# Another VectorE order in the folded down stages of a two-block fp32 network, and narrower weight panels

## The chip, the cores and the metric

One core of a Trainium2 chip runs the whole program. The metric is device time in microseconds (us); lower is better.

## What is computed

Two network blocks run one after the other on an fp32 activation of 512 tokens by 1024 features. The first is a gated mixer with a feed-forward layer, the second a short-convolution mixer, a forgetting attention and two convolutional feed-forward layers. The lines that matter here are the down projections of the feed-forward layers:

```python
h = rmsnorm(x, norm_ffn[l])
x = x + jnp.square(jax.nn.relu(h @ w_ff1[l])) @ w_ff2[l]
...
def conv_ffn(xn, w_up, conv_w, w_down):
    up = xn @ w_up
    a, g = jnp.split(up, 2, axis=-1)
    a = causal_dwconv(a, conv_w)
    return (jax.nn.silu(a) * g) @ w_down
```

The first layer has 4096 hidden features, each of the two others 2816.

## The kernel before

**Tiles and panels.** Activations lie transposed, 128 features by 512 tokens to a tile. Each fp32 operand is split in a high part (rounded to `fp32r`) and a low part (what is left), and a product takes three matmuls: high by high, high by low, low by high. The weights come as 353 panels of 128 x 1024. SyncE loads a panel into one of three slots (`w_raw`), ScalarE makes the high half (`high`, L478), GpSimd the low half (`low`, L433), TensorE reads both. ScalarE works `FEED` = 2 panels ahead. In the code `p0` is the first panel of a stage, and the stage's pair j has the panels p0 + 2j and p0 + 2j + 1.

**Folded down stages.** The hidden features are worked off in chunks of 8 tiles (the last chunk of each conv layer has 6): an up stage makes the hidden tiles, and a down stage adds their product to `x`. Eight of the down stages are folded (`FOLDED`): three of ff1, two of the first and three of the second conv layer. In such a stage two weight panels and the two halves of the tokens form a 2 x 2 block product, which is worked out with seven block products instead of eight. A stage has four pairs of panels (j = 0 to 3), so 28 blocks of 12 matmuls of 256 columns (9 in the last stage). For each pair:

- VectorE first makes four sums of weight quadrants. `sum_first` (L1069) overwrites a quadrant in `w_raw`, after ScalarE has copied the old one to PSUM (`copy_a21`, L523). `sum_third` (L1078) and `sum_rest` (L1084, L1086) write to PSUM. ScalarE makes the high halves of three of them (`high_of_sum`), VectorE the low halves (`low_of_sum`, L1092).
- TensorE works seven blocks. Blocks 1, 5 and 7 go to one PSUM accumulator, and between them VectorE must read it: `add_first` (L1147) after block 1, `add_second` (L1164) after block 5, `add_third` (L1182) after block 7. Block 5 waits for `add_first`, block 7 for `add_second`.
- Blocks 2 and 3 go to a second bank, read by `add_sides` (L1155, L1156), blocks 4 and 6 to a third, read by `add_crossing` (L1173). Block 4 of the next pair waits for the crossing.

All sums and additions are VectorE's, in an order that is written out by hand: `last_tile` has what comes with the last hidden tile and pair 0, `down_pairs` the rest. ScalarE's order is in its own `down_pairs`.

**The ring.** A load waits until the low half of the panel three before is made; the first panel of a pair is also a source of the sums, so the load over it (`load`, L388 to L392) waits for the pair's last sum. Since SyncE issues loads in order, the next one stands behind it:

```python
                    sp.wait_ge(w_low, p - RING + 1)
                    if PAIR_OF.get(p - RING, (0, 1))[1] == 0:
                        sp.wait_ge(s_made, 4 * PAIR_OF[p - RING][0] + 4)
```

So the sums of pair 1 gate the load of panel p0 + 5, the second of pair 2. On ScalarE and GpSimd a high or low half also waits until TensorE has read its slot (`wait_slot`).

Of the kernel before, what the change touches and what calls it, by code (L numbers as in the profile page):

```python
# [8 lines left out]
P = 128  # L9
SEQ = 512  # L10
D = 1024
DT = D // P
# [56 lines left out]
for _p in PAIRS:  # L69
    PAIR_OF[_p], PAIR_OF[_p + 1] = (PAIR_AT[_p], 0), (PAIR_AT[_p], 1)  # L70
WHOLE = [sum(1 for _i in range(_p + 1) if _i not in PAIR_OF) for _p in range(N_PANELS)]


B1_HIGH, T_HIGH, PART_LOW, REST_LOW = {}, {}, {}, {}
# [62 lines left out]
def build(nc, xT, panels, const, late, param, rows, ws, outT):  # L137
# [5 lines left out]
    with ctx:  # L143
# [241 lines left out]
        @block.sync  # L385
        def _(sp):
            def load(p):
                if p >= RING:  # L388
                    sp.wait_ge(w_low, p - RING + 1)
                    if PAIR_OF.get(p - RING, (0, 1))[1] == 0:  # L390
                        sp.wait_ge(s_made, 4 * PAIR_OF[p - RING][0] + 4)
                sp.dma_start(w_raw[:, p % RING, :], panels[p]).then_inc(w_in[p % RING], 16)  # L392

            sp.dma_start(params[:], param).then_inc(param_in, 16)
            for m in range(DT):
                sp.dma_start(x[:, m, :], xT[m]).then_inc(x_in[m], 16)
                if m == 0:
                    load(0)
            load(1)
            load(2)  # L400
            sp.dma_start(consts[:], const).then_inc(c_in, 16)
            for p in range(RING, N_PANELS):
                load(p)
                if p == RING + 1:
                    sp.dma_start(rows_sb, rows.partition_broadcast(P)).then_inc(row_in, 16)
                    sp.dma_start(ws_sb, ws).then_inc(row_in, 16)
                m = p - (S["upb"] + RING + 1)
                if 0 <= m < DT:

                    sp.wait_ge(evicted, S["upb"] + m + 1)  # L410
                    sp.dma_start(x[:, m, :], xT[m]).then_inc(x_again[m], 16)
                    if m == 0:
                        sp.dma_start(consts[:, LATE:LATE + N_LATE], late).then_inc(late_in, 16)
            for m in range(DT - 1):

                sp.wait_ge(evicted, N_PANELS - DT + m + 1)
                sp.dma_start(outT[m], x[:, m, :]).then_inc(out_done, 16)

            for part in range(2):
                at = slice(part * SEQ // 2, (part + 1) * SEQ // 2)  # L420
                sp.wait_ge(evicted, N_PANELS + part)
                sp.dma_start(outT[DT - 1][:, at], x[:, DT - 1, at]).then_inc(out_done, 16)
            sp.wait_ge(out_done, 16 * (DT + 1))

        @block.gpsimd
        def _(pool):
            def low(p):

                if p >= N_PANELS:
                    return  # L430
                pool.wait_ge(w_high, p + 1)
                wait_slot(pool, p)
                nc.gpsimd.tensor_tensor(w_lo[:, p % RING, :], w_raw[:, p % RING, :], w_hi[:, p % RING, :].bitcast(F),  # L433
                                        ALU.subtract).then_inc(w_low, 1)


            def low_t23(key, i):

                k2 = TILES_AT[key] // 2
                pool.wait_ge(t_high, T_HIGH[key] + k2 + 2 * i + 1)  # L440
                nc.gpsimd.tensor_tensor(t23_lo[:, i, :], keep[i], t23_hi[:, i, :].bitcast(F),
                                        ALU.subtract).then_inc(t23_low, 1)

            def low_t23_behind(p):

                for key in FOLDED:
                    p0, tiles = down_stage(*key)
                    k2 = tiles // 2
                    if key[0] == "ff1":
                        ready = {p0 - DT + 2 + m: m - 1 for m in range(5, 8)}  # L450
                        if p in ready:
                            low_t23(key, ready[p] - k2)
                        if p == p0 + 1:
                            low_t23(key, k2 - 1)
                    else:
                        m = (p - 3 - (p0 - 2 * tiles)) // 2
                        if p % 2 == (p0 + 1) % 2 and k2 <= m < tiles:
                            low_t23(key, m - k2)

            pool.wait_ge(x_low, DT)  # L460
            for p in range(N_PANELS):
                low(p)
                low_t23_behind(p)

        @block.scalar
        def _(act):
            steps = Steps(act, act_steps)

            def high(p):

                if p >= N_PANELS:
                    return
                if PAIR_OF.get(p, (0, 0))[1] == 1:
                    act.wait_ge(s_made, 4 * PAIR_OF[p][0] + 1)
                else:
                    act.wait_ge(w_in[p % RING], 16 * (p // RING + 1))
                wait_slot(act, p)
                nc.scalar.copy(w_hi[:, p % RING, :], w_raw[:, p % RING, :]).then_inc(w_high, 1)  # L478

            def split(dst, src, scale=None):  # L480
                return nc.scalar.activation(dst, src, ACT.Copy, scale=1.0 if scale is None else scale)  # L481
# [43 lines left out]
            def down_pairs(key):  # L525

                p0, tiles = down_stage(*key)
                for j in range(DT // 2):
                    p = p0 + 2 * j
                    more = j < DT // 2 - 1  # L530
                    if j > 0:
                        if more:
                            copy_a21(PAIR_AT[p + 2], tiles)
                        high(p + FEED)
                    high(p + FEED + 1)
                    if more:
                        for i in range(3):
                            high_of_sum(PAIR_AT[p + 2], i, tiles // 2 * P)
# [477 lines left out]
        def _(dve):  # L1016
# [126 lines left out]
            def add_first(p0, j):  # L1143
# [2 lines left out]
                dve.wait_ge(part_made, 7 * q + 1)  # L1146
                v.tensor_tensor(x[:, m, 0:HALF], x[:, m, 0:HALF], acc_of(p0, j), ALU.add).then_inc(acc_read, 1)  # L1147

            def add_sides(p0, j):

                q, m = PAIR_AT[p0 + 2 * j], 2 * j
                p5 = ps[:, SIDE_BANKS[0], HALF:SEQ]
                dve.wait_ge(part_made, 7 * q + 3)
                dve.wait_ge(acc_read, 2 * q + (1 if j > 0 else 2))
                v.tensor_tensor(x[:, m, :], x[:, m, :], ps[:, SIDE_BANKS[0], :], ALU.add).then_inc(side_read, 1)  # L1155
                v.tensor_tensor(x[:, m + 1, HALF:SEQ], x[:, m + 1, HALF:SEQ], p5, ALU.add).then_inc(side_read, 1)  # L1156

            def add_second(p0, j):

                q, m = PAIR_AT[p0 + 2 * j], 2 * j  # L1160
                dve.wait_ge(part_made, 7 * q + 5)
                if j > 0:
                    dve.wait_ge(side_read, 2 * q + 2)
                v.tensor_tensor(x[:, m, HALF:SEQ], x[:, m, HALF:SEQ], acc_of(p0, j), ALU.add).then_inc(acc_read, 1)  # L1164

# [23 lines left out]
            def last_tile(key, to):  # L1189

                p0, tiles = down_stage(*key)
                q, i, k2 = PAIR_AT[p0], tiles // 2 - 1, tiles // 2
                low_rest(key, i, to, k2)
                t2_t3(key, i, k2)
                if key[0] == "ff1":
                    low_of_sum(q, 0, tiles)
                low_of_sum(q, 1, tiles)
                add_first(p0, 0)
                t4(key, i, k2)
                sum_first(q + 1, tiles)  # L1200
                low_t4(key, i, k2)
                low_of_sum(q, 2, tiles)

            def down_pairs(key):

                p0, tiles = down_stage(*key)
                for j in range(DT // 2):
                    q = PAIR_AT[p0 + 2 * j]
                    more = j < DT // 2 - 1
                    if j == 0:  # L1210
                        add_second(p0, j)
                        add_sides(p0, j)
                        add_crossing(p0, j)
                        sum_third(q + 1, tiles)
                        sum_rest(q + 1, tiles)
                        low_of_sum(q + 1, 0, tiles)
                        low_of_sum(q + 1, 1, tiles)
                        continue
                    low_of_sum(q, 2, tiles)
                    add_third(p0, j - 1)  # L1220
                    if more:
                        sum_first(q + 1, tiles)
                    add_first(p0, j)
                    if more:
                        sum_third(q + 1, tiles)
                        sum_rest(q + 1, tiles)
                    add_sides(p0, j)
                    if more:
                        low_of_sum(q + 1, 0, tiles)
                    add_second(p0, j)  # L1230
                    if more:
                        low_of_sum(q + 1, 1, tiles)
                    add_crossing(p0, j)
# [1213 lines left out]
```

## Time and profile before

| | before |
|---|---|
| median of 3 runs | 2032.32 us (2031.04 to 2032.36) |
| profiled execution | 2033.78 us |
| its span | 2032.0 us |
| mean granted clock of TensorE | 0.997 |
| HBM read, written | 190.62 MB, 2.10 MB |
| loads of weight panels | 353 of 512 KB |

The span runs from the first to the last instruction; what lies around it is the start and the end of the execution. Times in the rows further on are microseconds from the start of the span.

### The profile page before, as it was taken

To read this page: it belongs to the slowest core of one execution; us is meant where nothing else is said; L and a number is where in the kernel's file an instruction comes from. 1 tells how busy PE (TensorE), PEld (TensorE's weight loads), DVE (VectorE), ACT (ScalarE), POOL (GpSimd) and SP (SyncE) were. 2 spreads that over 40 slices of the span, in tenths; PEclk is the share of its full clock that TensorE was granted. 3 is DMA by queue.
4 is the path that set the end of the run, shared out by engine and by line. 5 is a ranking of instruction groups with operands and counts; after the bars stand their busy time and mean duration, and the time that the engine had idled before them with its cause. 6 is when DMAs were issued, how large, how long until landed. Compare 5 with 4: busy or idle time off the path is not lost. (4 is left out here: it accounts for less than half of the span.)

```text
span 2032.0 us, 28871 instructions
## 1 busy us (share of the span) xinstructions
PE 2005.0 (99%) x11386; PEld 1696.0 (83%) x11386; DVE 1203.8 (59%) x1985; ACT 908.2 (45%) x1389; POOL 909.7 (45%) x388
## 2 busy tenths in 40 slices
PE   9999999999999999999999999999999999999998
PEld 7888888888889888888888889888877778888987
DVE  4688888634737454434457557454376746755657
ACT  6455556534534434512434234246377743423333
POOL 4334443644545444444445445454422234545544
PEclk9999999999999999999999999999999999999999
DMA  5222222433333232332322333332311122332323
GB/s 179 82 86 74 84 84 83 131 133 93 100 98 104 84 104 94 101 95 86 103 93 94 104 94 108 92 117 88 104 53 63 52 84 94 98 100 94 105 92 104
DMA packets 55286, 194.59 MB, mean 96 GB/s; under 512 B 6128, under 2 KB 6640, under 8 KB 55152
## 3 DMA queue, kind: packets, MB, share of 16 engines
q1 hardware_dynamic: 55152, 192.75, 29.7%
q8 instruction: 91, 1.49, 0.3%
q14 instruction: 43, 0.35, 0.1%
HBM read 190.62 MB, written 2.10 MB: 95 GB/s over the span
## 5 line engine op out<-in xcount | busy, mean ns | idle before, releaser
L433 POOL TENSOR_TENSOR w_lo<-w_raw,w_hi 128x1024 fp32r<-128x1024 f32 x353 | 869.9, 2470 | 1045.6 <-ACT w_hi L478 1029.3
L1860 PE MATMUL ps<-a_hi,w_hi 128*128 128x512 f32 x1152 | 456.4, 396 | 0.2 <-DVE x L1245 0.2
L1862 PE MATMUL ps<-a_hi,w_lo 128*128 128x512 f32 x1152 | 449.1, 390 | 0.0
L1861 PE MATMUL ps<-a_lo,w_hi 128*128 128x512 f32 x1152 | 448.8, 390 | 0.0
L478 ACT CAST w_hi<-w_raw 128x1024 fp32r<-128x1024 f32 x353 | 365.0, 1042 | 144.9 <-PE ps L1884 58.3
L1860 PE MATMUL ps<-b_hi,w_hi 128*128 128x512 f32 x1000 | 390.1, 390 | 0.2 <-DVE x L1245 0.2
L1862 PE MATMUL ps<-b_hi,w_lo 128*128 128x512 f32 x1000 | 389.1, 389 | 0.0
L1861 PE MATMUL ps<-b_lo,w_hi 128*128 128x512 f32 x1000 | 389.0, 389 | 0.0
L1034 DVE TENSOR_TENSOR arena<-ps,inv_rms 128x512 f32<-128x512 f32 x176 | 121.4, 690 | 309.6 <-PE ps L1862 292.0
L1860 PEld LDWEIGHTS ps<-a_hi,w_hi 128*128 128x128 f32 x1152 | 216.3, 188 | 47.8 <-issue 2.8
L1861 PEld LDWEIGHTS ps<-a_lo,w_hi 128*128 128x128 f32 x1152 | 216.4, 188 | 45.7 <-issue 2.2
L1862 PEld LDWEIGHTS ps<-a_hi,w_lo 128*128 128x128 f32 x1152 | 216.2, 188 | 45.3
L1860 PEld LDWEIGHTS ps<-b_hi,w_hi 128*128 128x128 f32 x1000 | 187.7, 188 | 39.8 <-issue 1.0
L1862 PEld LDWEIGHTS ps<-b_hi,w_lo 128*128 128x128 f32 x1000 | 187.7, 188 | 39.2
L1861 PEld LDWEIGHTS ps<-b_lo,w_hi 128*128 128x128 f32 x1000 | 187.7, 188 | 38.8 <-issue 0.2
L481 ACT ACTIVATE a_hi<-arena 128x256 fp32r<-128x256 f32 (+1 forms) x70 | 35.0, 508 | 169.9 <-DVE arena L1634 67.1
L845 ACT ACTIVATE ps<-ps 128x512 f32<-128x512 f32 x44 | 25.6, 582 | 186.0 <-DVE ps L1625 186.0
L481 ACT ACTIVATE s_hi<-ps 128x512 fp32r<-128x512 f32 (+1 forms) x96 | 52.7, 584 | 95.2 <-PE ps L1884 48.5
L1882 PE MATMUL ps<-t_hi,s_hi 128*128 128x256 f32 x248 | 72.1, 291 | 19.7 <-DVE x L1147 14.6
L1092 DVE TENSOR_TENSOR s_lo<-ps,s_hi 128x512 fp32r<-128x512 f32 (+1 forms) x96 | 62.7, 669 | 33.1 <-ACT s_hi L481 33.1
L1883 PE MATMUL ps<-t_lo,s_hi 128*128 128x256 f32 x248 | 70.8, 286 | 0.0
L1884 PE MATMUL ps<-t_hi,s_lo 128*128 128x256 f32 x248 | 70.3, 284 | 0.0
(277 smaller groups left out, 3142.1 us busy)
## 6 DMA issues: line engine op xcount, KB each, us to landing
w_raw<-in_panels SPq DMA_DIRECT2D x353, 512.0 KB, 3.6
x<-in_xT SPq DMA_DIRECT2D x16, 256.0 KB, 2.8
outT<-x SPq DMA_DIRECT2D x7, 256.0 KB, 3.1
consts<-in_const SPq DMA_DIRECT2D x1, 528.5 KB, 8.2
arena<-in_rows SPq DMA_DIRECT2D x1, 256.0 KB, 4.6
arena<-in_ws SPq DMA_DIRECT2D x1, 256.0 KB, 5.1
outT<-x SPq DMA_DIRECT2D x2, 128.0 KB, 1.8
consts<-in_late SPq DMA_DIRECT2D x1, 168.0 KB, 2.6
```

Of the source, the lines that this page charges most:

```text
L433: nc.gpsimd.tensor_tensor(w_lo[:, p % RING, :], w_raw[:, p % RING, :], w_hi[:, p % RING, :].bitcast(F), ALU.subtract).then_inc(w_low, 1)
L478: nc.scalar.copy(w_hi[:, p % RING, :], w_raw[:, p % RING, :]).then_inc(w_high, 1)
L481: return nc.scalar.activation(dst, src, ACT.Copy, scale=1.0 if scale is None else scale)
L845: nc.scalar.activation(hidden(m), hidden(m), ACT.Silu).then_inc(silu_done, 1)
L1034: return v.tensor_tensor(dst, bank(p), inv_rms[:, :], ALU.mult)
L1092: v.tensor_tensor(s_lo[:, i, 0:h], ps[:, S_BANKS[i], 0:h], s_hi[:, i, 0:h].bitcast(F), ALU.subtract).then_inc(s_low, 1)
L1860: nc.tensor.matmul(o, wh, hi[:, kt, :], start=(kt == 0), stop=False)
L1861: nc.tensor.matmul(o, wh, lo[:, kt, :], start=False, stop=False)
L1862: ins = nc.tensor.matmul(o, wl, hi[:, kt, :], start=False, stop=(kt == tiles - 1))
L1882: nc.tensor.matmul(o, wh, rh, start=(first and kt == 0), stop=False, skip_group_check=not first)
L1883: nc.tensor.matmul(o, wh, rl, start=False, stop=False, skip_group_check=not first)
L1884: ins = nc.tensor.matmul(o, wl, rh, start=False, stop=(kt == k2 - 1), skip_group_check=not first)
```

## The change

There are three parts. `COLS` gives each panel a width: the 16 panels of the two 6-tile down stages get 768 columns in place of 1024, in the load, the high half and the low half. ScalarE's order in pair 1 gets `high(p + FEED)` ahead of `copy_a21`. And VectorE's order changes in pairs 0, 1 and 2 of each folded stage.

```diff
+COLS = [D] * N_PANELS
+for _l, _n in [(_l, _n) for _l in range(2) for _n in range(len(FF2_CHUNKS))]:
+    _p0, _tiles = down_stage(f"ffn_{_l}", _n)
+    COLS[_p0:_p0 + DT] = [_tiles * P] * DT
...
-                sp.dma_start(w_raw[:, p % RING, :], panels[p]).then_inc(w_in[p % RING], 16)
+                sp.dma_start(w_raw[:, p % RING, 0:COLS[p]], panels[p][:, 0:COLS[p]]).then_inc(w_in[p % RING], 16)
...
-                    if j > 0:
+                    if j == 1:
+                        high(p + FEED)
+                        copy_a21(PAIR_AT[p + 2], tiles)
+                    elif j > 0:
                         if more:
                             copy_a21(PAIR_AT[p + 2], tiles)
                         high(p + FEED)
...
+            def sides_first(p0, j):
+                return j > 0 or p0 < S["conv_b"]
...
                 add_first(p0, 0)
                 t4(key, i, k2)
+                if sides_first(p0, 0):
+                    add_sides(p0, 0)
                 sum_first(q + 1, tiles)
                 low_t4(key, i, k2)
                 low_of_sum(q, 2, tiles)
...
                     if j == 0:
                         add_second(p0, j)
+                        sum_third(q + 1, tiles)
+                        sum_rest(q + 1, tiles)
+                        if not sides_first(p0, j):
+                            add_sides(p0, j)
+                        low_of_sum(q + 1, 0, tiles)
+                        add_crossing(p0, j)
+                        low_of_sum(q + 1, 1, tiles)
+                        continue
+                    low_of_sum(q, 2, tiles)
+                    add_third(p0, j - 1)
+                    if more:
+                        add_first(p0, j)
+                        sum_first(q + 1, tiles)
                         add_sides(p0, j)
-                        add_crossing(p0, j)
+                        add_second(p0, j)
                         sum_third(q + 1, tiles)
                         sum_rest(q + 1, tiles)
                         low_of_sum(q + 1, 0, tiles)
                         low_of_sum(q + 1, 1, tiles)
+                        add_crossing(p0, j)
                         continue
-                    low_of_sum(q, 2, tiles)
-                    add_third(p0, j - 1)
```

Pair 3 keeps its order. `sides_first` is true in pair 0 of the ff1 stages only (and in all later pairs).

VectorE in the first folded stage, from `add_first` of pair 0 to `add_second` of pair 1. Before:

```order
570 L1147 TENSOR_TENSOR x<-x,ps 128x256 [waits part_made]
...
575 L1164 TENSOR_TENSOR x<-x,ps 128x256 [waits part_made]
576 L1155 TENSOR_TENSOR x<-x,ps 128x512 [waits acc_read,part_made]
577 L1156 TENSOR_TENSOR x<-x,ps 128x256
578 L1173 TENSOR_TENSOR x<-x,ps 128x512 [waits side_read,acc_read,part_made]
579 L1078 TENSOR_TENSOR ps<-w_raw,ps 128x512 [waits s_low,w_in0]
...
583 L1182 TENSOR_TENSOR x<-x,ps 128x512 [waits evicted,part_made]
584 L1069 TENSOR_TENSOR w_raw<-w_raw,ps 128x512 [waits a21_copied]
585 L1147 TENSOR_TENSOR x<-x,ps 128x256 [waits part_made]
586 L1078 TENSOR_TENSOR ps<-w_raw,ps 128x512 [waits s_low,w_in2]
...
592 L1164 TENSOR_TENSOR x<-x,ps 128x256 [waits side_read,part_made]
```

And in the changed kernel, where the same operations have other line numbers (`add_first` L1157, `sum_first` L1079, sides L1168 and L1169, `add_second` L1177, crossing L1186, `add_third` L1195):

```order
570 L1157 TENSOR_TENSOR x<-x,ps 128x256 [waits part_made]
...
572 L1168 TENSOR_TENSOR x<-x,ps 128x512 [waits acc_read,part_made]
573 L1169 TENSOR_TENSOR x<-x,ps 128x256
...
577 L1177 TENSOR_TENSOR x<-x,ps 128x256 [waits side_read,part_made]
578 L1088 TENSOR_TENSOR ps<-w_raw,ps 128x512 [waits s_low,w_in0]
...
582 L1186 TENSOR_TENSOR x<-x,ps 128x512 [waits side_read,acc_read,part_made]
...
585 L1157 TENSOR_TENSOR x<-x,ps 128x256 [waits part_made]
586 L1079 TENSOR_TENSOR w_raw<-w_raw,ps 128x512 [waits a21_copied]
...
589 L1177 TENSOR_TENSOR x<-x,ps 128x256 [waits side_read,part_made]
590 L1088 TENSOR_TENSOR ps<-w_raw,ps 128x512 [waits s_low,w_in2]
```

The sides of pair 0 moved to the front, its crossing behind the sums; in pair 1 `add_first` and `sum_first` changed places, and `add_second` moved ahead of the sums.

ScalarE in the same stage, from the high halves of pair 1's sums on. Before:

```order
384 L481 ACTIVATE s_hi<-ps 128x512 [waits part_made,s_made] x3
385 L523 COPY ps<-w_raw 128x512 [waits s_low,w_in0]
386 L478 CAST w_hi<-w_raw 128x1024 [waits part_made,w_in2]
387 L478 CAST w_hi<-w_raw 128x1024 [waits part_made,s_made]
388 L481 ACTIVATE s_hi<-ps 128x512 [waits part_made,s_made] x3
```

Changed:

```order
384 L488 ACTIVATE s_hi<-ps 128x512 [waits part_made,s_made] x3
385 L485 CAST w_hi<-w_raw 128x1024 [waits part_made,w_in2]
386 L530 COPY ps<-w_raw 128x512 [waits s_low,w_in0]
387 L485 CAST w_hi<-w_raw 128x1024 [waits part_made,s_made]
388 L488 ACTIVATE s_hi<-ps 128x512 [waits part_made,s_made] x3
```

The cast of panel p0 + 4 moved ahead of the copy out of panel p0 + 5.

## Rows read from the trace of the kernel before

**Rows 1.** The page: busy us, share of the span and instructions of each engine.
```profile
PE 2005.0 (99%) x11386; PEld 1696.0 (83%) x11386; DVE 1203.8 (59%) x1985; ACT 908.2 (45%) x1389; POOL 909.7 (45%) x388
```

**Rows 2.** Timeline of TensorE: start us, us, instruction, idle before and its releaser.
```profile
527.16 0.28 PE L1882 MATMUL ps<-a_hi,w_hi 128*128 128x256 f32 x1
...
531.36 0.28 PE L1884 MATMUL ps<-a_hi,w_lo 128*128 128x256 f32 x1
...
545.46 0.38 PE L1882 MATMUL ps<-t_hi,s_hi 128*128 128x256 f32 x1 [1.90 <-DVE x L1147]
...
1114.79 0.36 PE L1882 MATMUL ps<-t_hi,s_hi 128*128 128x256 f32 x1 [1.22 <-DVE x L1147]
...
2008.61 0.36 PE L1882 MATMUL ps<-t_hi,s_hi 128*128 128x256 f32 x1 [2.71 <-DVE x L1147]
```

**Rows 3.** TensorE's waits, whole span: us in total, times, longest us.
```profile
PE ps L1882 <- DVE x L1147: 14.6, 8, 2.7
PE ps L1882 <- DVE x L1164: 4.7, 7, 0.8
...
PE ps L1882 <- POOL w_lo L433: 0.6, 1, 0.6
```

**Rows 4.** The eight folded down stages, TensorE alone: stretch, us, busy us (instructions), clock.
```profile
527.16:571.18 44.02, 42.02 (x336) 0.96 0.35 112
...
1992.04:2028.63 36.59, 32.67 (x252) 0.95 0.34 116
sum 339.15, PE 318.84; mean PE 39.86
```

**Rows 5.** Stretches behind four waits: PE, PEld, DVE, ACT, POOL busy, clock, DMA share, GB/s.
```profile
545.60:549.00 3.40, 3.40 (x17) 3.40 (x18) 3.33 (x7) 1.78 (x3) 3.40 (x2) 0.51 0.20 19
634.40:637.80 3.40, 3.40 (x18) 3.40 (x18) 3.23 (x7) 1.08 (x2) 3.38 (x2) 0.50 0.37 106
718.80:722.20 3.40, 1.15 (x10) 0.98 (x9) 1.99 (x4) 2.51 (x3) 1.00 (x1) 1.00 0.28 113
2010.00:2013.40 3.40, 3.08 (x15) 2.81 (x14) 2.90 (x7) 0.87 (x2) 3.33 (x2) 0.50 0.43 69
```

**Rows 6.** Timeline of VectorE in the first folded stage, and one row of the fourth.
```profile
534.06 0.69 DVE L1069 TENSOR_TENSOR w_raw<-w_raw,ps 128x512 f32<-128x512 f32 x1 [1.31 <-ACT ps L523]
...
535.60 0.41 DVE L1164 TENSOR_TENSOR x<-x,ps 128x256 f32<-128x256 f32 x1
...
537.87 0.69 DVE L1078 TENSOR_TENSOR ps<-w_raw,ps 128x512 f32<-128x512 f32 x1
...
540.68 1.89 DVE L1092 TENSOR_TENSOR s_lo<-ps,s_hi 128x512 fp32r<-128x512 f32 x3 [0.66 <-ACT s_hi L481]
...
544.90 0.41 DVE L1147 TENSOR_TENSOR x<-x,ps 128x256 f32<-128x256 f32 x1
...
1105.03 0.42 DVE L1164 TENSOR_TENSOR x<-x,ps 128x256 f32<-128x256 f32 x1
```

**Rows 7.** Timeline of ScalarE in the first folded stage.
```profile
543.67 0.59 ACT L523 COPY ps<-w_raw 128x512 f32<-128x512 f32 x1 [2.04 <-DMA w_raw<-in_panels]
544.20 1.99 ACT L478 CAST w_hi<-w_raw 128x1024 fp32r<-128x1024 f32 x2
```

**Rows 8.** Timeline of GpSimd in the first folded stage.
```profile
545.31 4.74 POOL L433 TENSOR_TENSOR w_lo<-w_raw,w_hi 128x1024 fp32r<-128x1024 f32 x2 [7.00 <-ACT w_hi L478]
```

**Rows 9.** Timeline of the last folded stage: GpSimd, then `sum_first` of pair 2 on VectorE.
```profile
1996.37 1.29 POOL L441 TENSOR_TENSOR t_lo<-arena,t_hi 128x512 fp32r<-128x512 f32 x1 [4.55 <-ACT t_hi L481]
1997.62 4.73 POOL L433 TENSOR_TENSOR w_lo<-w_raw,w_hi 128x1024 fp32r<-128x1024 f32 x2
...
2007.58 0.55 DVE L1069 TENSOR_TENSOR w_raw<-w_raw,ps 128x384 f32<-128x384 f32 x1 [2.01 <-ACT ps L523]
```

**Rows 10.** DMA issues: KB each, median us from issue to landing.
```profile
w_raw<-in_panels SPq DMA_DIRECT2D x353, 512.0 KB, 3.6
x<-in_xT SPq DMA_DIRECT2D x16, 256.0 KB, 2.8
```

More of the change, by code:

```diff
@@ L430, in low @@
                     return
+                n = COLS[p]
                 pool.wait_ge(w_high, p + 1)
                 wait_slot(pool, p)
-                nc.gpsimd.tensor_tensor(w_lo[:, p % RING, :], w_raw[:, p % RING, :], w_hi[:, p % RING, :].bitcast(F),
+                nc.gpsimd.tensor_tensor(w_lo[:, p % RING, 0:n], w_raw[:, p % RING, 0:n], w_hi[:, p % RING, 0:n].bitcast(F),
                                         ALU.subtract).then_inc(w_low, 1)
@@ L477, in high @@
                 wait_slot(act, p)
-                nc.scalar.copy(w_hi[:, p % RING, :], w_raw[:, p % RING, :]).then_inc(w_high, 1)
+                nc.scalar.copy(w_hi[:, p % RING, 0:COLS[p]], w_raw[:, p % RING, 0:COLS[p]]).then_inc(w_high, 1)
             def split(dst, src, scale=None):
@@ L1153, in add_sides @@
                 dve.wait_ge(part_made, 7 * q + 3)
-                dve.wait_ge(acc_read, 2 * q + (1 if j > 0 else 2))
+                dve.wait_ge(acc_read, 2 * q + (1 if sides_first(p0, j) else 2))
                 v.tensor_tensor(x[:, m, :], x[:, m, :], ps[:, SIDE_BANKS[0], :], ALU.add).then_inc(side_read, 1)
@@ L1161, in add_second @@
                 dve.wait_ge(part_made, 7 * q + 5)
-                if j > 0:
+                if sides_first(p0, j):
                     dve.wait_ge(side_read, 2 * q + 2)
```

## The prediction

> **What bounds the kernel now.** The page first: TensorE is busy for 2005.0 of 2032.0 us, VectorE 59%, ScalarE and GpSimd 45% [rows 1]. Only what delays TensorE counts, and the busy share hides part of it: records of 256-column matmuls last 0.28 us but start 0.12 apart (35 steps from 527.16 to 531.36), so each idle time in the records hides another 0.16 [rows 2].
>
> Then TensorE's own waits: 14.6 us in 8 waits for the first addition (`add_first`, L1147), 4.7 in 7 for the second (`add_second`, L1164), 0.6 for a low half of GpSimd, all before a block of a folded down stage (L1882) [rows 3]. With what they hide that is 19.9 + 16 x 0.16 = 22.5. The Trainium skill (Trainium Kernel Development and Optimization, the note on reading a trace) calls matmul busy time a bad metric because matmuls are pipelined; whoever goes by it sees 19.9, and a sum 2.6 smaller.
>
> Third, the eight folded down stages as stretches, 339.15 us together [rows 4]. They hold 7 x 336 + 252 = 2604 matmuls, 312.5 us at 0.12: **26.7 us** are lost in them. The difference from 22.5 is the clock. Behind three of the L1147 waits the granted clock is 0.50 (the level of 1.2 GHz): 17 and 18 matmuls in 3.4 us, where 28 fit at 2.4 GHz, so 10 or 11 x 0.12 = 1.3 us each, 3.9 for three. In the third stage the clock stays at 1.00 through a like wait [rows 5]. 22.5 + 3.9 = 26.4, so the two counts agree.
>
> **Why it stalls.** In the first stage VectorE ends the sums of pair 1 at 540.02 (540.68 less 0.66 of idle) [rows 6]. That releases the load of pair 2's second panel (`load`, L390); it lands 3.6 us later, and ScalarE copies a quadrant of it at 543.67 [rows 7]. `sum_first` waits for the copy, and only behind it comes `add_first`, at 544.90. TensorE goes on at 545.46, 0.56 later, after 1.90 idle; it was ready at 545.46 - 1.90 - 0.16 = 543.40 [rows 2, 6]. The second wait, of 0.8, comes before block 7 of the same pair: `add_second` stands behind three sums, two side additions and a low half.
>
> **The change, part by part.**
>
> *First addition of pair 1.* It now stands ahead of `sum_first`, so neither load nor copy gates it. In the first stage the sums start behind `add_second`, at 535.60 + 0.41 = 536.0 where 537.87 stood, take 2.15 as before (537.87 to 540.02) and end at 538.2. Then 0.66 for ScalarE, low half 0.63, crossing 0.69, two low halves 1.26, `add_third` 0.69: `add_first` starts by 542.1, TensorE may go by 542.7, and wants to at 543.4 [rows 6]. In the ffn stages the side additions come behind the sums, 0.69 + 0.41 in place of the 0.66: from `add_second` at 1105.03, 0.41 + 2.15 + 1.10 + 0.63 + 0.69 + 1.26 + 0.69 gives 1112.0, and TensorE may go at 1112.5; it wants to at 1114.79 - 1.22 - 0.16 = 1113.4 [rows 2, 6]. Slack 0.7 and 0.9, so in seven stages the wait goes: 14.6 - 2.7 = 11.9, plus 7 x 0.16: **13.0**.
>
> *Sides first in ff1.* They now run ahead of pair 1's `sum_first`, which sat idle for 1.31 waiting for the copy [rows 6]; 1.10 of work fits. Cost 0. Were that cover gone, up to 1.1 would show before block 7 of pair 0 in each of three stages.
>
> *Second additions of pairs 1 and 2* now precede the next pair's sums. In pair 1 block 5 starts at 543.4 and ends 12 x 0.12 = 1.44 later; wake-up about 0.2 (an estimate from TensorE's own, 0.56 - 0.41), addition and hand-over 0.56: 545.6, where block 7 wants it at 546.3. Five such waits of 0.8 go: 4.2 + 5 x 0.16 = **5.0**.
>
> What stands behind that new wait: the next pair's sums, low halves and crossing, and through the sums a panel load. From a pair's start: block 5 ends at 7.2, then 0.2 + 0.41 + 2.15, so 10.0; load 3.6; copy and `sum_first`, 544.90 - 543.67 = 1.2; cast 1.0; GpSimd 2.4: 18.2 [rows 6 to 8]. It is wanted at the second block of the pair after next, 2 x 10.1 + 1.4 = 21.6. Covered by 3.4, so 0.
>
> *ScalarE's swap.* The cast of pair 2's first panel no longer waits for the copy (544.20 [rows 7]); it comes before the third low half, by 540.8, so GpSimd has it from about 541.8 and not from 545.31 [rows 8]. This matters: two panels take 4.74, and unswapped the second would be ready at 550.05 while TensorE, 2 us ahead, wants it at 547.5 + 1.4 = 548.9. Swapped, it is loaded by 541.8, summed by 543.2, cast by 544.3 and split by 546.7.
>
> *Narrower panels.* 16 loads, casts and low halves shrink to 768 columns. Eight serve a down stage where TensorE doesn't wait: 0. Eight serve the last stage, whose pairs take 84 x 0.75 x 0.12 = 7.6. No row has this width. GpSimd does 1024 columns in 2.4 and 512 in 1.3 [rows 8, 9]; these are the bounds, and I take 1.85, halfway. 512 KB land in 3.6, 256 KB in 2.8 [rows 10]; I take 3.2. The low half that costs 0.6 is the second of the two from 1997.62 [rows 9]; with 1.0 less it is on time: 0.7. In `add_first`'s path the idle of 2.01 and the 0.55 of `sum_first` [rows 9] go and the sides fill 0.66 of idle, so it comes about 3.2 earlier, at 2004.9, TensorE may go at 2005.4; it wants to at 2008.61 - 2.71 - 0.16 less the 1.0 saved before it, 2004.7. So 0.7 stays of 2.9: 2.2. The short second waits: 0.5. Every cover is under 1 us in this stage; I give back 0.3: **3.1**.
>
> *The clock.* The three drops follow waits that go: **3.9**.
>
> Sum 13.0 + 5.0 + 3.1 + 3.9 = 25.0. The profiled execution took 2033.8 (span 2032.0): 2008.8. The runs' median is 1.5 lower, 2032.3: **2007.3**.
>
> **The rivals.**
> - *A, as above*: 0.80. Its ends: all 26.7 go and the step is a little under 0.12, 2004; or 4 us of new waits of a few tenths, 2011.
> - *B, the clock drops stay*: 0.07. Something other than these waits sets them, since the wait of the third stage has none behind it [rows 5]. Against it: there are three in 2032 us, all in stages with a wait of 1.9 or more. Price 3.9: 2011.2. The Trainium skill (TensorE: Matmul & The Clock Gate, The HAM clock gate) has the clock fall when the array was idle; by the letter, an array that works between its waits would not qualify, and the drops would stay.
> - *C, one wait takes another's place*: 0.08. First additions are on time, but GpSimd's low half (4.74 in a row [rows 8]) or a second addition comes 1.0 late in two pairs of each stage, as the second waits did: 16 back, 2023. Against it: the swap.
> - *D, slower*: 0.02. VectorE now stands at `add_second` until block 5 ends, with all sums behind it. Were the chain of 18.2 to run over 21.6, each further microsecond would stall 16 pairs. It decides at 3.4 longer; at 6 longer it costs 16 x 2.6 = 42, less the 25 gained: 2049.
> - *E, no effect*: 0.03. The waits move on to the load, whose release still hangs on the sums; about 2032. Against it: those sums come 1.9 earlier.
>
> **How the numbers follow.** A measurement of this kernel tells 0.2%, 4.1 us, from no change. A, B and C are faster, 0.95; E the same, 0.03; D slower, 0.02. The range leaves out D, E and most of C: 2003.5 to 2016. A's own is 2004 to 2011.
>
> **What would show it.** The seven full down stages last 40.3 to 40.8 us and the last about 32; no L1147 wait over 0.8; no granted clock of 0.50 inside the span; `sum_first` of pair 2 starts behind `add_first`; GpSimd splits pair 2's panels apart. I am wrong if TensorE waits for `w_lo` in pair 2, if L1164's waits stay, or if half clock appears without a wait.

## The result and the profile after

| | before | changed |
|---|---|---|
| median | 2032.34 us | 2006.98 us |
| lowest to highest of 4 runs | 2031.04 to 2032.65 | 2005.84 to 2007.18 |
| ratio of the two, 95% interval | | 0.9875 (0.9858 to 0.9892) |
| profiled execution, its span | 2033.78, 2032.0 | 2005.84, 2004.1 |

The medians lie 25.4 us apart; the forecast was 25.0 less, 2007.3. The profiled executions lie 27.9 apart, because that of before is above its median and that of the changed kernel below. A second measurement of the changed kernel (e9 further on) came out 26.2 below the kernel before.

The page of the changed kernel, which answers to [rows 1]:

```profile
span 2004.1 us, 28874 instructions
...
PE 1996.7 (100%) x11386; PEld 1690.9 (84%) x11386; DVE 1200.4 (60%) x1985; ACT 902.4 (45%) x1389; POOL 900.7 (45%) x388
```

TensorE's busy time fell from 2005.0 to 1996.7 though it runs the same matmuls. Matmuls at half clock were recorded longer (0.41 us in place of 0.28), and ahead of each wait the last record counts in full, where the next one otherwise starts 0.12 into it.

The folded down stages, TensorE alone (stretch, its us, busy us with the count, granted clock, DMA share, GB/s), which answer to [rows 4]:

```profile
526.40:566.61 40.21, 40.21 (x337) 1.00 0.37 123
610.26:650.40 40.14, 40.14 (x336) 1.00 0.37 122
694.07:734.28 40.21, 40.21 (x337) 1.00 0.36 122
1085.32:1125.20 39.88, 39.88 (x337) 1.00 0.37 124
...
1968.79:2000.69 31.90, 31.19 (x252) 1.00 0.34 112
sum 311.98, PE 311.27; mean PE 38.91
```

The three between 1125 and 1968 also last 39.88. The first three stages, those of ff1, last 0.3 longer than 39.88. The sum fell from 339.15 to 311.98, so 27.2 of the 27.9 us of span came from these stages. In seven of them TensorE is never idle by the records, and the clock is 1.00 in all.

TensorE's waits from 1968 to 2001, in the last stage, are the only ones that the records show in a folded stage:

```profile
PE ps L1909 <- DVE x L1177: 0.3, 1, 0.3
PE ps L1909 <- POOL t_lo L448: 0.2, 1, 0.2
PE ps L1909 <- DVE x L1169: 0.2, 1, 0.2
```

Then the first stage step by step. VectorE, ScalarE and GpSimd, each in a block of its own, to be held against [rows 6 to 8]:

```profile
535.02 0.69 DVE L1088 TENSOR_TENSOR ps<-w_raw,ps 128x512 f32<-128x512 f32 x1
...
540.83 0.41 DVE L1157 TENSOR_TENSOR x<-x,ps 128x256 f32<-128x256 f32 x1
541.47 0.69 DVE L1079 TENSOR_TENSOR w_raw<-w_raw,ps 128x512 f32<-128x512 f32 x1 [0.22 <-ACT ps L530]
...
544.10 0.42 DVE L1177 TENSOR_TENSOR x<-x,ps 128x256 f32<-128x256 f32 x1 [1.02 <-PE ps L1911]
```

```profile
538.65 1.06 ACT L485 CAST w_hi<-w_raw 128x1024 fp32r<-128x1024 f32 x1
540.84 0.59 ACT L530 COPY ps<-w_raw 128x512 f32<-128x512 f32 x1 [1.13 <-DMA w_raw<-in_panels]
```

```profile
539.79 2.40 POOL L440 TENSOR_TENSOR w_lo<-w_raw,w_hi 128x1024 fp32r<-128x1024 f32 x1 [2.39 <-PE ps L1911]
543.32 2.39 POOL L440 TENSOR_TENSOR w_lo<-w_raw,w_hi 128x1024 fp32r<-128x1024 f32 x1 [1.13 <-ACT w_hi L485]
```

And TensorE at blocks 5 and 7 of pair 1:

```profile
542.48 0.28 PE L1909 MATMUL ps<-t_hi,s_hi 128*128 128x256 f32 x1
...
545.30 0.29 PE L1909 MATMUL ps<-t_hi,s_hi 128*128 128x256 f32 x1
```

The sums start at 535.02 (537.87 before), the copy comes at 540.84 (543.67), and `add_first` at 540.83 (544.90), now ahead of `sum_first`. TensorE could have gone at 541.4 (540.83 and the 0.56 of the hand-over) and went when it was ready, at 542.48: slack 1.1. VectorE then stands for 1.02 at `add_second`, which is the new wait; it costs TensorE nothing, since 544.10 + 0.56 is 0.6 ahead of 545.30. GpSimd splits pair 2's two panels at different times, at 539.79 and at 543.32, and no longer in a row.

The loads of 384 KB landed in a median of 3.2 us:

```profile
w_raw<-in_panels SPq DMA_DIRECT2D x337, 512.0 KB, 3.6
w_raw<-in_panels SPq DMA_DIRECT2D x16, 384.0 KB, 3.2
```

### The profile page after: what moved, and what is told of

It reads as the page before. It is cut to its first block, busy times and chain, and to the rows that moved or that the text cites. A ratio compares the mean times of both kernels' runs of the same rounds, so it can differ in the third digit from the quotient of the medians.

```text
span 2004.1 us, 28874 instructions
## 1 busy us (share of the span) xinstructions
PE 1996.7 (100%) x11386; PEld 1690.9 (84%) x11386; DVE 1200.4 (60%) x1985; ACT 902.4 (45%) x1389; POOL 900.7 (45%) x388
## 4 chain that ended last, share of the span: by engine, by line
PE 97%; DVE 1%; DMA 1%; issue 0%; SPq 0%; ACT 0%; DVEq 0%; ACTq 0%
PE ps L1887 25%; PE ps L1889 25%; PE ps L1888 25%; PE ps L1909 5%; PE ps L1910 5%; PE ps L1911 5%; PE ps L2318 1%; PE ps L2284 1%; PE ps L2309 1%; PE ps L2243 1%; PE ps L2242 1%; PE ps L2241 1%; DMA w_raw<-in_panels 1%; PE ps L2085 1%; PE ps L1953 0%; PE ps L1983 0%
## 5 line engine op out<-in xcount | busy, mean ns | idle before, releaser
L440 POOL TENSOR_TENSOR w_lo<-w_raw,w_hi 128x1024 fp32r<-128x1024 f32 (+1 forms) x353 | 860.8, 2443 | 1026.3 <-ACT w_hi L485 990.9
L485 ACT CAST w_hi<-w_raw 128x1024 fp32r<-128x1024 f32 (+1 forms) x353 | 362.0, 1033 | 130.2 <-PE ps L1889 45.9
L1887 PEld LDWEIGHTS ps<-b_hi,w_hi 128*128 128x128 f32 x1000 | 187.7, 188 | 39.9 <-issue 1.0
L448 POOL TENSOR_TENSOR t_lo<-arena,t_hi 128x512 fp32r<-128x512 f32 x31 | 40.1, 1295 | 67.1 <-ACT t_hi L488 67.1
```

Of the source, the lines that this page charges most:

```text
L440: nc.gpsimd.tensor_tensor(w_lo[:, p % RING, 0:n], w_raw[:, p % RING, 0:n], w_hi[:, p % RING, 0:n].bitcast(F), ALU.subtract).then_inc(w_low, 1)
L485: nc.scalar.copy(w_hi[:, p % RING, 0:COLS[p]], w_raw[:, p % RING, 0:COLS[p]]).then_inc(w_high, 1)
L1887: nc.tensor.matmul(o, wh, hi[:, kt, :], start=(kt == 0), stop=False)
```

## The experiments

Each run has the kernel before beside it on the same chip; its median was 2033.15 in the first group (e1 to e4), 2032.62 in the second (e5 to e8) and 2032.63 in the third (e9, e10). "e5: before" means the kernel before with that edit, "e1: changed" the changed kernel with it. "Stages" is the sum over the eight folded stages in the profile, 339.15 before and 311.98 changed.

| run | median us | against before | stages |
|---|---|---|---|
| e1: changed, ScalarE's old order | 2006.31 | -26.8 | 311.83 |
| e2: changed, old pair 0 | 2011.33 | -21.8 | 316.92 |
| e3: changed, late second additions | 2012.47 | -20.7 | 317.79 |
| e4: changed, with delays (one run) | 2023.68 | | 328.36 |
| e5: before, `add_first` ahead | 2034.81 | +2.2 | 338.53 |
| e6: before, new pair 0 | 2015.92 | -16.7 | 322.07 |
| e7: changed, wide panels | 2008.47 | -24.2 | 314.20 |
| e8: changed, sides early in the last stage | 2006.22 | -26.4 | 311.88 |
| e9: changed, again | 2006.39 | -26.2 | |
| e10: e8 and a second swap | 2005.53 | -27.1 | 311.73 |

### One edit alone: the wait moves

**e5** puts `add_first` ahead of `sum_first` and leaves all else of the kernel before. It does so in pairs 1 to 3; pair 3 has no `sum_first`, so only pairs 1 and 2 change:

```diff
-                    if more:
-                        sum_first(q + 1, tiles)
                     add_first(p0, j)
+                    if more:
+                        sum_first(q + 1, tiles)
```

> The kernel before with one edit: in pairs 1 to 3 add_first stands ahead of sum_first; all else old. Theory: the load and the copy leave add_first's path, so the first waits fall from 1.9 us to about 0.2 in ff1 (add_first at 543.1, TensorE at 543.7, wanted at 543.4), the clock drops go too, but the copy, the cast and the low half of pair 2's second panel are where they were (550.05) while TensorE wants it at 548.9: a wait for w_lo of about 1.1 takes its place, and the second waits of 0.8 grow to about 1.5 to 2. About 2032 - 13 - 4 + 8 x 2 = 2031 to 2024. If nothing takes their place: 2032 - 17 = 2015.

Measured: 2034.81, ratio 1.0015 (1.0006 to 1.0025), outside the expected 2024 to 2031 and not faster at all. The profiled execution was the fastest of ten (2032.56 to 2039.51). VectorE, then TensorE, in the first stage:

```profile
542.62 0.41 DVE L1151 TENSOR_TENSOR x<-x,ps 128x256 f32<-128x256 f32 x1
544.00 0.69 DVE L1073 TENSOR_TENSOR w_raw<-w_raw,ps 128x512 f32<-128x512 f32 x1 [0.96 <-ACT ps L527]
...
546.05 0.69 DVE L1090 TENSOR_TENSOR ps<-w_raw,ps 128x512 f32<-128x512 f32 x1
...
548.19 0.41 DVE L1171 TENSOR_TENSOR x<-x,ps 128x256 f32<-128x256 f32 x1
```

```profile
548.75 0.36 PE L1891 MATMUL ps<-t_hi,s_hi 128*128 128x256 f32 x1 [2.49 <-DVE x L1171]
```

Its waits over the whole span:

```profile
PE ps L1891 <- DVE x L1171: 20.0, 10, 3.0
```

`add_first` came 2.3 us earlier than before, and TensorE's records show no wait before block 5 of pair 1. But `sum_first` still waited for the load, and behind it stand three sums, the sides, a low half and then `add_second`, at 548.19. So the 19.3 us of both additions' waits became 20.0 of the second's alone. The expected waits of about 1.1 for `w_lo` did not come; only the 0.6 of the last stage is there, as before. In the other stages TensorE was held up ahead of it.

**e6** is the other half alone, the new order of pair 0 (with the sides ahead in ff1), in the kernel before:

```diff
                         add_second(p0, j)
-                        add_sides(p0, j)
-                        add_crossing(p0, j)
                         sum_third(q + 1, tiles)
                         sum_rest(q + 1, tiles)
+                        if not sides_first(p0, j):
+                            add_sides(p0, j)
                         low_of_sum(q + 1, 0, tiles)
+                        add_crossing(p0, j)
                         low_of_sum(q + 1, 1, tiles)
```

> The kernel before with the new order in pair 0 only (sides and crossing behind the sums of pair 1, in ff1 the sides ahead of sum_first). The sums end 1.9 us earlier, so load, copy, sum_first and add_first come 1.9 us earlier, as long as the load isn't held by GpSimd: first waits fall by 1.9 in ff1 (all of it) and by 1.2 to 1.5 in the ffn stages (all of it), the last keeps about 1. Then the waits before block 7 of pair 1 stay or grow to 1 to 2, since add_second stands behind the sums: 2032 - 14 - 4 + 0 to 8 = 2014 to 2022. If pair 1's order is what counts, less than 5 us is gained: 2027 or more.

Measured: 2015.92, inside the expected 2014 to 2022, so the new order of pair 0 alone brings 16.7 us. Its granted clock is 1.00 in all eight stages, so this holds the three clock drops too. The waits left:

```profile
PE ps L1892 <- DVE x L1171: 6.5, 10, 1.0
...
PE ps L1892 <- DVE x L1151: 0.5, 2, 0.3
```

`sum_first` of pair 2 in the first stage, in the kernel before and in e6:

```profile
544.29 0.69 DVE L1069 TENSOR_TENSOR w_raw<-w_raw,ps 128x512 f32<-128x512 f32 x1 [1.13 <-ACT ps L523]
```

```profile
542.13 0.69 DVE L1073 TENSOR_TENSOR w_raw<-w_raw,ps 128x512 f32<-128x512 f32 x1 [0.82 <-ACT ps L527]
```

It starts 2.2 us earlier, and with it all that stands behind. The first additions' waits shrink from 14.6 to 0.5, though `add_first` still stands behind the copy.

**e2** is the complement: the changed kernel without the new pair 0 (the diff above reversed, and `sides_first` false there).

> The changed kernel with the old order in pair 0 (second addition, sides, crossing, then the sums of pair 1); pairs 1 and 2 keep the new order. If the reordering of pairs 1 and 2 alone takes the load off the first addition's path, add_first of pair 1 starts at about 542.3 + 0.7 us and TensorE waits about 0.2 before block 5, and another 0.2 to 0.5 before block 7, since sum_first and the sides are 1.9 us later: +0.3 to 0.7 per full stage, +1.5 in the last, 2007 + 3 to 6 = 2010 to 2013. If the earlier sums of pair 1 carry most of the gain, the first waits of 1.2 to 2.7 come back: 2007 + 13 = 2020.

Measured: 2011.33, inside the 2010 to 2013 of the first theory. One wait for a first addition is left, in the last stage:

```profile
PE ps L1908 <- DVE x L1157: 0.6, 1, 0.6
```

The run gives back 4.4 of e9's 26.2. The new order of pairs 1 and 2 (with the swap and narrow panels) thus brings 21.8 on its own, and the new pair 0 brings 16.7: together 26.2, not 38.5. Either part takes the late load and copy off TensorE's path, and what is left after one of them is small.

**e3** keeps everything of the changed kernel but the place of `add_second` in pairs 1 and 2:

```diff
                         add_first(p0, j)
                         sum_first(q + 1, tiles)
-                        add_sides(p0, j)
-                        add_second(p0, j)
                         sum_third(q + 1, tiles)
                         sum_rest(q + 1, tiles)
+                        add_sides(p0, j)
                         low_of_sum(q + 1, 0, tiles)
+                        add_second(p0, j)
                         low_of_sum(q + 1, 1, tiles)
                         add_crossing(p0, j)
```

> The changed kernel with add_second of pairs 1 and 2 back behind the next pair's sums, the sides and a low half. By the prediction the second additions are worth 5.0 us: five waits of 0.8 before block 7 of pair 1, so 2012. Worked out from the rows of the changed kernel it is more: the sums start at 542.2, end at 544.3, sides 545.4, low half 546.1, add_second 546.1, TensorE may go at 546.7 and wants to at 545.3 in pair 1: 1.4 per stage and the like in pair 2, up to 8 x 2 x 1.4 = 22, 2029. If the new wait for block 5 costs anything (sums later), this run would be faster than that.

Measured: 2012.47, which gives back 5.5 of e9's 26.2, each against the kernel before beside it. That is near the prediction's 5.0 and far from the 22 worked out from the changed kernel's rows. `add_second` of pair 1 in the first stage, and TensorE's waits for it over the whole span:

```profile
546.33 0.41 DVE L1177 TENSOR_TENSOR x<-x,ps 128x256 f32<-128x256 f32 x1
```

```profile
PE ps L1909 <- DVE x L1177: 4.3, 8, 1.3
```

These are eight waits, one a stage; in the first stage it stands before block 7 of pair 1, and none stands in pair 2. The larger estimate carried pair 1's wait over to pair 2 without working out pair 2's own chain.

### What the swap and the narrow panels are worth

**e1** undoes ScalarE's swap:

```diff
-                    if j == 1:
-                        high(p + FEED)
-                        copy_a21(PAIR_AT[p + 2], tiles)
-                    elif j > 0:
+                    if j > 0:
```

> The changed kernel with ScalarE's old order in pair 1 (copy ahead of the cast of panel p0+4). As the prediction put it, the swap is needed: GpSimd's two low halves of pair 2 then run in a row, the second comes 1.1 us late in each of 8 stages, and the time is about 2007 + 8 = 2015, with TensorE waiting for w_lo. The rival: the prediction left out that the copy itself now comes 2.8 us earlier (540.84 where 543.67 stood), so the row of 4.7 us ends by 547.3 where TensorE wants the second low half at 547.9; then nothing changes in seven stages, up to 0.3 in the last, and the time is 2007.

Measured: 2006.31, no slower than the changed kernel. GpSimd does run the two low halves in a row, but earlier than before:

```profile
543.09 4.77 POOL L440 TENSOR_TENSOR w_lo<-w_raw,w_hi 128x1024 fp32r<-128x1024 f32 x2 [5.11 <-ACT w_hi L485]
```

They end at 547.9. The stage starts at 527.04 and TensorE wants the second one 20.1 + 1.4 later, at about 548.6. TensorE's records show no wait for `w_lo` anywhere in this run. The rival holds: the swap is worth nothing that the times or the stages show.

**e7** gives all panels back their 1024 columns (`COLS = [D] * N_PANELS`).

> The changed kernel with all panels 1024 columns wide. Seven folded stages and the unfolded down stage don't change. In the last stage GpSimd takes 2.4 us for a low half and not 1.85, so the second one of pair 1 comes about 1 us late (a wait of 0.6 to 1.0 for w_lo), the load of pair 2's second panel lands about 0.5 later, and pairs 2 and 3 each wait some tenths: +1.5 to +3 in all, 2008.5 to 2010. Rival: the narrower panels are hidden in this stage too (its waits were VectorE's), 2007.

Measured: 2008.47, 2.1 more than e9 and at the lower end of what was expected. The seven full stages are as in the changed kernel, the last is longer by 2.1, 34.01 against 31.90:

```profile
1969.17:2003.18 34.01, 31.62 (x252) 1.00 0.39 124
```

In it TensorE waits for GpSimd again:

```profile
PE ps L1906 <- POOL w_lo L437: 1.6, 2, 1.0
PE ps L1906 <- DVE x L1174: 0.5, 1, 0.5
```

### The clock

**e4** makes VectorE late in the changed kernel: reductions whose results nothing uses stand ahead of `add_first` of pair 1, another number in each stage.

```diff
+                        if j == 1:
+                            for n in range(DELAYS[FOLDED.index(key)]):
+                                at = 8 * FOLDED.index(key) + n
+                                v.tensor_reduce(spare[:, at:at + 1], consts[:, 0:SEQ], AX.X, ALU.max)
```

> The changed kernel with 3, 4, 5, 6, 7, 8, 5 and 0 extra reductions on VectorE (128x512, about 0.55 us each, their results unused) ahead of add_first of pair 1 in the eight folded stages. Theory of the prediction: TensorE waits for add_first by what exceeds a slack of about 1.5 us, so 0 to 3 us, and the granted clock falls to 0.5 behind waits of about 2 us and more, not behind shorter ones and nowhere else. Rival B: the drops have another cause, then they come in stages without such a wait or not at all.

TensorE at block 5 of pair 1 in the third to the sixth stage (start us, us, instruction, idle before):

```profile
714.36 0.36 PE L1917 MATMUL ps<-t_hi,s_hi 128*128 128x256 f32 x1 [1.70 <-DVE x L1161]
...
1107.41 0.36 PE L1917 MATMUL ps<-t_hi,s_hi 128*128 128x256 f32 x1 [1.89 <-DVE x L1161]
...
1238.71 0.36 PE L1917 MATMUL ps<-t_hi,s_hi 128*128 128x256 f32 x1 [2.48 <-DVE x L1161]
...
1766.08 0.36 PE L1917 MATMUL ps<-t_hi,s_hi 128*128 128x256 f32 x1 [3.08 <-DVE x L1161]
```

and stretches behind the last three of these waits (us, TensorE's busy us with the count, clock, DMA share, GB/s):

```profile
1108.00:1111.20 3.20, 3.20 (x17) 0.50 0.02 5
1239.00:1242.20 3.20, 3.20 (x29) 1.00 0.02 5
1766.80:1770.00 3.20, 3.20 (x17) 0.50 0.00 0
```

The waits were 0.5, 1.1, 1.7, 1.9, 2.5, 3.1 and 1.3 in stage order. Half clock followed the waits of 1.9 and 3.1, in stages that had no drop before, and no other wait in the stages, not even that of 2.5. The first, the second and the last stage had a drop before and have no wait of 1.9 here; no drop came there. So in these runs drops go with long waits, and rival B falls. But not every long wait has one. In the kernel before, the third stage kept its clock of 1.00 [rows 5] through this wait:

```profile
721.34 0.36 PE L1882 MATMUL ps<-t_hi,s_hi 128*128 128x256 f32 x1 [2.25 <-DVE x L1147]
```

What decides it these runs leave open, but it is not the program alone. The ten runs of e5 are one program on one chip, and they reach from 2032.56 us at a mean granted clock of 0.998 to 2039.51 at 0.994: the less clock, the longer. So executions of one program differ in their number of drops, and e5's 2.2 us over the kernel before are in part such drops.

The price can be read off the fourth to the seventh stage of e4, of which the fifth and the seventh have no drop:

```profile
1089.62:1133.14 43.52, 41.63 (x336) 0.96 0.34 112
1220.32:1262.90 42.58, 40.09 (x337) 1.00 0.35 115
1747.09:1791.81 44.72, 41.64 (x336) 0.96 0.34 110
1878.99:1920.40 41.41, 40.11 (x336) 1.00 0.35 118
```

The fifth is 39.88 + 2.48 + 0.22, the seventh 39.88 + 1.30 + 0.23. So a wait hides 0.23 and not only 0.16: the next matmul behind it also starts 0.19 after the first one, where 0.12 is the step. The fourth is then 39.88 + 1.89 + 0.23 + 1.52, and the sixth 39.88 + 3.08 + 0.23 + 1.53. **A drop cost 1.5 us**, not 1.3.

### A slightly faster version

**e8** takes the two VectorE waits out of the last stage:

```diff
-                return j > 0 or p0 < S["conv_b"]
+                return j > 0 or p0 < S["conv_b"] or p0 > N_PANELS - 16
...
-                        sum_first(q + 1, tiles)
-                        add_sides(p0, j)
+                        if p0 > N_PANELS - 16 and j == 2:
+                            add_sides(p0, j)
+                            sum_first(q + 1, tiles)
+                        else:
+                            sum_first(q + 1, tiles)
+                            add_sides(p0, j)
```

> The changed kernel with the sides of pair 0 ahead of sum_first in the last stage too, and the sides of pair 2 ahead of sum_first there. It removes TensorE's wait for add_sides (0.21 idle, 0.37 with its hidden part) at block 2 of pair 1 and that for add_second (0.27, 0.43) at block 7 of pair 2, if sum_first isn't delayed by more than its idle time (0.66 and 0.76 for 0.93 of work): -0.5 us, 2006.5, which the measurement can hardly tell; the profile of the last stage should last 31.4 and not 31.9. If sum_first's delay of 0.3 comes through, nothing is gained.

Measured: 2006.22, and a last stage of 31.40 as expected. A gain that small is not told from e9 by the times (2005.96 to 2006.42 here, 2005.88 to 2006.59 there).

**e9** is the changed kernel once more:

> The changed kernel itself once more, beside the next one and with five rounds: 2006 to 2007, one half-clock stretch at most, behind the last matmul. It says how far runs of one kernel differ between chips and sessions.

Measured: 2006.39 (2005.88 to 2006.59). Its last stage took 31.55 (1969.08 to 2000.63) and not 31.90, and has no wait for `add_second`. So the last stage alone varies by some 0.3 between executions, and against e9 e8's gain in it is 0.15, not 0.5.

**e10** adds the swap of ScalarE in pair 2 of the last stage:

```diff
-                    if j == 1:
+                    if j == 1 or j == 2 and tiles < DT:
```

> The kernel of the sides run, and in the last stage ScalarE's swap in pair 2 also (the cast of pair 3's first panel ahead of the copy). The sides run left waits of 0.54 (GpSimd's second low half of pair 3) and 0.52 (a low half of an activation) in the last stage. The first goes: the last stage lasts 31.0 where the changed kernel has 31.9, so 0.9 less than the changed kernel, 0.05%, which five rounds may or may not tell. Rival: GpSimd's first low half collides with nothing but the sum's path delays sum_first, and the wait before block 7 of pair 2 comes back: 31.4.

Measured: 2005.53 (2005.43 to 2005.73) beside e9's 2005.88 to 2006.59, with four runs each. The two don't overlap. The medians lie 0.9 us apart, and it is the lowest of all. One wait is left in its last stage that the records show:

```profile
PE ps L1913 <- POOL t_lo L448: 0.2, 1, 0.2
```

The stage lasted 31.26, not 31.0. The profiled executions of the two kernels differ by 0.27 us (2005.61 and 2005.88), and the last stage (31.26 and 31.55) accounts for that. The other 0.6 between the medians shows in no trace: how much of the 0.9 is the edit's stays open.

## Why the prediction was right, and where not

- **What bounds the kernel, and how much is lost.** The right place, but three sizes were off. Taking 0.12 for a step was slightly too long: a stage without a wait lasted 39.88, that is 0.119 a step. Seven such stages and one of three quarters would be 309.1, so 30.1 us were lost in 339.15 and not 26.7. Each wait hid 0.23, not 0.16, and each drop cost 1.5, not 1.3. 27.2 us went and 2.9 are left, 2.0 in the last stage and 0.9 in the three of ff1. For the same reason the full stages lasted 39.9 to 40.2, not 40.3 to 40.8. That the counts of 26.4 and 26.7 agreed was luck: with these sizes they are 28.2 and 30.1.
- **First additions, 13.0, and second additions, 5.0.** Right as a sum, but as separate terms they mislead. e3's 5.5 is near the 5.0, partly by luck: it comes of eight waits, one a stage, and the 5.0 of five. The text credited 13.0 to `add_first` standing ahead of `sum_first`; e5 shows that this edit alone gains nothing, since the whole wait moves to `add_second`. It was the same chain (sums, load, copy, `sum_first`), seen twice. Two things release it: both additions ahead of the next pair's sums (e2, 21.8, with the swap and the narrow panels), or sums of pair 1 that start earlier in pair 0 (e6, 16.7).
- **Slack.** `add_first` was worked out for 542.1 with 0.7 of slack in the first stage; it came at 540.83 in a stage that began 0.8 earlier, with 1.1. The bounds (durations in place of the shorter steps between starts) were on the safe side.
- **Sides first, cost 0.** Right: by the steps between matmuls the three stages of ff1 lost 0.1 to 0.2 before block 7 of pair 0, where they had lost 0.2 to 0.5 before.
- **The new wait's queue, 0.** Right in the seven full stages. VectorE stands 1.02 at `add_second` in the first, and nothing behind it became late. Rival D had no part.
- **ScalarE's swap.** This step failed, without a trace in the number. The text had the second low half of pair 2 ready at 550.05 without the swap, and called the swap needed. It took over the time of the old kernel for a copy that the rest of the change brings forward: from 543.67 to 540.84, 2.8 us, of which 0.8 is the stage's own earlier start. e1 has the low half ready at 547.9, 0.7 before it is wanted, and loses nothing.
- **Narrow panels and the last stage, 3.1.** The stage went from 36.59 to 31.90, 4.7, of which about 1.5 is a clock drop: 3.2. The price of the panels was not given by itself; e7 says 2.1. GpSimd took 1.85 for 768 columns and the load 3.2 us, as chosen between the bounds.
- **The clock, 3.9.** Right in kind: the three drops went with the waits, and e4 brought two back with waits. The size was 4.6, three times 1.53. Counting 17 or 18 matmuls in 3.4 us took in those at the edges; in e4's drops 16 steps of 0.21 stand in place of 0.119, which is 1.5.
- **The total.** 25.0 against 25.4 and, measured again, 26.2. In the profiles the stages gave back 27.2: the drops and what each wait hides were sized too low by some 1.7 us together, and the first measurement of the changed kernel lies 0.6 above the second. That 25.0 came within 0.4 is in part luck.
- **The rivals.** B did not come: the clock is 1.00 in every folded stage. C came true only in e5, in one edit's kernel; E is nearly what e5 shows (2034.8), through `add_second` and not through the load itself.

## What to carry to other kernels

When an in-order engine is late at one instruction, write down everything between the late input and the last consumer that the bound engine waits for. Moving only the first consumer ahead can gain nothing; moving all of them ahead of the late input, or bringing the input forward, does. And price each part of a change against the timeline that the other parts leave: gains of parts that shorten one chain don't add (16.7 and 21.8 made 26.2), and a safeguard that the old timeline calls for may be idle in the new one. Idle time of TensorE in the records is understated, here by 0.23 us a wait, and some waits (the shortest was 1.89 us) cost 1.5 more through the clock.

## What was not expected of the hardware

Of the waits of 1.9 us and more seen in folded stages, some were followed by half clock (1.90, 2.08, 2.71 before; 1.89 and 3.08 in e4) and some not (2.25 before; 2.48 in e4; six of e5's eight, which were 2.1 to 3.0 long). The length of the wait alone doesn't tell, and executions of one program differ (e5, 0.994 to 0.998 of mean clock). No wait of 0.2 to 1.7 us in a folded stage, in the kernel before or in e4, was followed by half clock.
